# Another layout of the differential attention, with the rotary cosine product on GpSimd

## The reference, cut to what matters

```
q = rope(rms_norm(q, q_g)); k = rope(rms_norm(k, k_g))     # q, k: [tokens, 8 heads, 2, 64]
ky = rms_norm(ky, k_g)                                      # context keys: no rope
s = einsum('bqhcd,bkhcd->bhcqk', q, keys)                   # two components c
p = softmax(s / 8)
a = p[:, :, 0] - lam * p[:, :, 1]
o = einsum('bhqk,bkhe->bqhe', a, vals)                      # vals: 128 wide
out = (rms_norm(o, sub_g) * 0.8).reshape(n, 1024) @ w_o
rope: t1 * cos - t2 * sin, t2 * cos + t1 * sin
```

## Time and profile before

| | us |
|---|---|
| median of 3 runs | 3831.35 (3828.03 to 3834.58) |
| profiled execution, its own time | 3833.75 |
| its span, first to last instruction | 3832.0 |
| PE busy | 3579.2 (93%) |
| DVE busy | 1932.7 (50%) |
| ScalarE busy | 1272.9 (33%) |
| GpSimd busy | 350.1 (9%) |
| mean granted TensorE clock | 0.948 |

### The profile page before, as it was taken

One profiled execution on the slowest core, in us unless ns is written; L12 is line 12 of the kernel. 1 busy time (PEld: TensorE's weight loads), 2 busy tenths in 40 slices (PEclk: granted clock), 3 DMA queues, 4 the chain that ended last, 5 costly groups with the idle time before them and its releaser, 6 DMA issues.

```text
span 3832.0 us, 40505 instructions
## 1 busy us (share of the span) xinstructions
PE 3579.2 (93%) x17064; PEld 2949.4 (77%) x17064; DVE 1932.7 (50%) x2742; ACT 1272.9 (33%) x1771; POOL 350.1 (9%) x200
## 2 busy tenths in 40 slices
PE   2999998899998999899999999989999999999998
PEld 2888887677776888788877888766788877678887
DVE  8434334455555544454444333386564647656464
ACT  4322123333333322322333323333442433344242
POOL 3301001000101000000000000330100023010001
PEclk9999998888888999999999999998899999899999
DMA  5323232000002545354322222220122222012221
GB/s 194 135 84 127 89 116 72 33 28 28 28 34 91 185 147 170 118 173 154 116 77 81 96 99 94 85 79 6 51 98 99 95 77 84 6 50 88 99 94 60
DMA packets 95654, 348.83 MB, mean 91 GB/s; under 512 B 10608, under 2 KB 10864, under 8 KB 94960
## 3 DMA queue, kind: packets, MB, share of 16 engines
q1 hardware_dynamic: 94176, 343.06, 26.2%
q10 hardware_dynamic: 1296, 3.18, 0.2%
HBM read 344.10 MB, written 2.10 MB: 90 GB/s over the span
## 4 chain that ended last, share of the span: by engine, by line
PE 85%; DVE 9%; ACT 3%; POOL 1%; issue 1%; DMA 0%; ACTq 0%; SPq 0%; DVEq 0%; POOLq 0%
PE PS L325 84%; DVE CAC L1689 2%; DVE WL L1319 1%; PE PS L394 1%; DVE ST L1560 1%; ACT WH L845 1%; DVE SCR L1346 1%; POOL SM L1974 1%; ACT G L1012 0%; DVE X L1661 0%; ACT HH L896 0%; DVE ST L1780 0%; ACT G L884 0%; DVE X L1670 0%; POOL PTF L1967 0%
## 5 line engine op out<-in xcount | busy, mean ns | idle before, releaser
L325 PE MATMUL PS<-HH,WH 128*128 128x512 f32 (+1 forms) x3120 | 1204.5, 386 | 58.3 <-DVE HL L1676 18.1
L1319 DVE TENSOR_TENSOR WL<-RAW,WH 128x1024 fp32r<-128x1024 f32 x462 | 576.7, 1249 | 1261.5 <-ACT WH L845 1261.4
L325 PE MATMUL PS<-HL,WH 128*128 128x512 f32 (+1 forms) x3120 | 1187.8, 381 | 0.0
L325 PE MATMUL PS<-HH,WL 128*128 128x512 f32 (+1 forms) x3120 | 1183.1, 379 | 0.0
L845 ACT ACTIVATE WH<-RAW 128x1024 fp32r<-128x1024 f32 x496 | 524.4, 1057 | 1472.7 <-PE PS L325 1460.4
L325 PEld LDWEIGHTS PS<-HH,WH 128*128 128x128 f32 x3120 | 603.0, 193 | 183.7 <-DVE HL L1421 19.4
L325 PEld LDWEIGHTS PS<-HL,WH 128*128 128x128 f32 x3120 | 602.5, 193 | 113.7 <-issue 7.0
L325 PEld LDWEIGHTS PS<-HH,WL 128*128 128x128 f32 x3120 | 599.8, 192 | 111.1
L325 PE MATMUL PS<-AH,WH 128*128 128x512 f32 x1392 | 525.2, 377 | 0.0
L325 PE MATMUL PS<-AL,WH 128*128 128x512 f32 x1392 | 524.8, 377 | 0.0
L325 PE MATMUL PS<-AH,WL 128*128 128x512 f32 x1392 | 523.5, 376 | 0.0
(11 more groups left out here) (266 smaller groups left out, 3321.5 us busy)
## 6 DMA issues: line engine op xcount, KB each, us to landing
RAW<-wst SPq DMA_DIRECT2D x640, 512.0 KB, 3.3
X<-xT SPq DMA_DIRECT2D x1, 2048.0 KB, 12.3
out<-X SPq DMA_DIRECT2D x8, 256.0 KB, 2.0
PTF<-cb SPq DMA_DIRECT2D x1, 1024.0 KB, 4.9
Y<-yT SPq DMA_DIRECT2D x1, 1024.0 KB, 6.3
PTF<-cb ACTq DMA_DIRECT2D x1, 1024.0 KB, 4.8
HM<-sg ACTq DMA_DIRECT2D x4, 256.0 KB, 3.6
ROPE<-rope SPq DMA_DIRECT2D x1, 512.0 KB, 4.2
```

Of the source, the lines that this page charges most:

```text
L325: return e.matmul(o, l, r, start=start, stop=stop)
L1319: e.tensor_tensor(lo, raw_block(s), f32(hi), ALU.subtract).then_inc(*did("dve_done", ("wlo", b)))
```

## The change

PE: the banks of the attention are now given by number (`hold`), not in turn. Scores of a step lie in banks 0 to 2 as one tile of 128x1536; the matmuls of the two components, which use rows 0 to 63 and 64 to 127 of the array, alternate. The turned probabilities (and turned V, and K's spread) use banks 3 and 4, projections bank 5 (K also 6), sums of squares, permutations and spreads of O bank 6, the values' output bank 7. Pieces of the next head are placed anew: K at qt 0 (V's turn in its middle), K's sum, Q and K's permutation at qt 1, Q's sum, a third of V (256 columns), Q's permutation and K's spread at qt 2, the other 512 columns of V at qt 3. The first head starts with K, then Q, then V, and K of head 1 stands ahead of its scores. Cut to the core:

```diff
+            def scores(n):
+                _, prior = hold(("s", n), 768, 0)
+                _, more = hold(("s", n), 512, 2)
+                o = bank["s", n] = PS[:, 0:1536]
...
+                for i, (a, b) in enumerate(((0, 0), (0, 1), (1, 0))):
+                    m = mm(o[:, 512:768], Q[0][a], K[0][b][:, 512:768], i == 0, i == 2)
+                    if i == 2:
+                        m.then_inc(*did("pe_done", ("s bank 1", n)))
+                    mm(o[:, 1024:1536], Q[1][a], K[1][b][:, 256:768], i == 0, i == 2)
+                for i, (a, b) in enumerate(((0, 0), (0, 1), (1, 0))):
+                    m = mm(o[:, 0:512], Q[0][a], K[0][b][:, 0:512], i == 0, i == 2)
...
+                    q.wait_ge("s bank 1", n)
+                    m = mm(o[:, 768:1024], Q[1][a], K[1][b][:, 0:256], i == 0, i == 2)
...
+                if H < 8:
+                    if qt == 0 and n:
+                        project(("k", H), weights(1024, H), 0, NT, 5, True, lambda: turn_values(h))
+                    if qt == 1:
+                        key_stat(H)
+                        project(("q", H), weights(0, H), 0, NX, 5, True, lambda: key_permute(H))
+                    if qt == 2:
+                        query_stat(H)
+                        v = weights(2048, H)
+                        project(("v2", H), v, NX, NT, 5, False, lambda: query_permute(H, 6))
+                        key_spread(H, 3)
+                        if h:
+                            out_stat(h - 1)
+                        if H == 7:
+                            project(("v", H), v, 0, NX, 5)
+                    if qt == 3:
+                        if h:
+                            out_spread(h - 1)
+                        if H < 7:
+                            project(("v", H), v, 0, NX, 5)
```

The tail: output 7 (its first six eighths) stands before the last values; the last two eighths of outputs 0 to 5 run together, with the last sum and spread between their two halves:

```diff
+            turn_p(31)
+            lin([output(7, 0, 6)], oxs(0, 6), [5])
+            values(7, 1)
+            lin([output(m, 6, 8) for m in range(6)], oxs(6, 8), [0, 1, 2, 3, 4, 5], {1: last})
```

DVE: one maximum and one scaling for both components; the negation needs both. The splits of Q and K stand apart from their rotation, and the splits of O 0 to 5 come together at n = 27:

```diff
+            def row_max(n):
+                e.tensor_reduce(s8[:, 0:2], bank["s", n].rearrange("p (c k) -> p c k", c=2), AXX, ALU.max)
+                e.scalar_tensor_tensor(out=s8[:, 2:4], in0=s8[:, 0:2], scalar=-1.0, in1=r, op0=ALU.mult, op1=ALU.mult)
...
                 combine(n)
+                    if qt == 0 and n:
+                        v_split(h)
+                        stream(upto["v", h])
                     if qt == 1:
+                        k_rotate(H)
+                        stream(upto["k", H])
                     if qt == 2:
+                        q_rotate(H)
+                        stream(upto["q", H])
+                        k_scale(H)
+                            stat(("o", h - 1), 1, 4, 1.0 / 128, 1e-6)
+                        k_split(H)
                     if qt == 3:
+                        q_split(H)
+                            o_scale(h - 1)
```

ScalarE: the evictions of the next head stand ahead of the two exponentials of a step, for tiles that PE finished in the step before; the high half of P, weight blocks and splits stand behind them:

```diff
+                if qt == 0 and n:
+                    v_evict(h)
+                    if qt == 1:
+                        k_evict(H)
+                    if qt == 2:
+                        q_evict(H)
+                    if qt == 3:
+                        v_evict2(H)
+                softmax(n)
+                if n:
+                    p_split(n - 1)
```

GpSimd and DVE: the product with the cosine goes from `rope` to GpSimd, in place, behind the permutation that reads the same tile:

```diff
+        def by_cos(key, s):
+            kind, h = key
+            q.wait_ge("rope in")
+            q.wait_ge(kind + "s", h)
+            q.wait_ge("tile", ("p" + kind, h))
+            e.tensor_tensor(s, s, COS, ALU.mult).then_inc(*did("pool_done", ("ropea", key)))
+            def rotate(s, tile, t2, key, done):
+                e.tensor_tensor(t2, bank[tile], SIN, ALU.mult)
+                q.wait_ge("ropeb", key)
+                q.wait_ge("ropea", key)
+                e.tensor_tensor(s, s, t2, ALU.add)
```

More of the change, by code:

```diff
@@ L295, in take @@
             pos += n
[L296 to L299 removed]
+            return hold(name, 512 * n, i)
         def allowed():
@@ L328, in W, with lin @@
             return [((name, l, r0, c0, nr, ncol, dc),)]
-        def lin(tiles, xs):
+        def lin(tiles, xs, into=None, between={}):
             nonlocal released
-            taken = [take(name, N) for name, _, N in tiles]
+            taken = [hold(t[0], t[2], into[i]) if into else take(t[0], t[2]) for i, t in enumerate(tiles)]
             K = len(xs)
             for k, (hi, lo, step, rows) in enumerate(xs):
+                if k in between:
+                    between[k]()
                 for (name, units, N), (bk, prior) in zip(tiles, taken):
@@ L386, in spread, with turn @@
             m.then_inc(*did("pe_done", ("tile", ("sp", name)), ("smfree", name), *more))
-        def turn(name, src, nt, step, *more):
-            bk, prior = take(name, nt * 128)
+        def turn(name, src, nt, step, *more, into=None):
+            bk, prior = take(name, nt * 128) if into is None else hold(name, nt * 128, into)
             q.wait_ge(*step)
             for p in prior:
-                q.wait_ge("free", p)
+                q.wait_ge(*p)
             for t in range(nt):
@@ new lines, in project @@
+            def project(name, us, c0, c1, into, final=True, between=None):
+                nonlocal released
+                bk, prior = hold(name, c1 - c0, into)
+                q.wait_ge("wlo", us[0][2])
+                for p in prior:
+                    q.wait_ge(*p)
+                for k, (hi, lo, step, _) in enumerate(xs):
+                    q.wait_ge(*step)
+                    if k == 4 and between:
+                        between()
+                    for c in range(c0, c1, 512):
+                        d = min(c + 512, c1)
+                        o = bk[:, c - c0:d - c0]
+                        mm(o, us[k][0], hi[:, c:d], k == 0, False)
+                        mm(o, us[k][0], lo[:, c:d], False, False)
+                        m = mm(o, us[k][1], hi[:, c:d], False, k == 7)
+                steps = [("tile", name)]
+                if final:
+                    steps.append(("wfree", us[0][2]))
+                    released += 1
+                m.then_inc(*did("pe_done", *steps))
+                upto[name] = allowed()
@@ L524, in attention @@
-            values(7, 1)
-            stat(("o", 7), [(OSQ, 128, ones, ("osq", 7))], 4, 1)
-            spread(("o", 7), 4, None, ("rs", ("o", 7)), ("attention done",))
-            lin([output(m, 6, 8) for m in range(4)], oxs(6, 8))
-            for m in range(4, 8):
-                lin([output(m, 6, 8)], oxs(6, 8))
+                    turn_p(n - 1)
+                if H < 8:
[18 more added lines that the diff above has]
+                            project(("v", H), v, 0, NX, 5)
+                else:
+                    if qt == 0:
+                        turn_values(7)
+                    if qt == 2:
+                        out_stat(6)
+                    for m in ((0, 1), (2, 3), (4, 5), (6,))[qt]:
+                        lin([output(m, 0, 6)], oxs(0, 6), [5])
+                        if m == 4:
+                            out_spread(6)
@@ L531, in fourier, with last @@
+            turn_p(31)
+            lin([output(7, 0, 6)], oxs(0, 6), [5])
+            values(7, 1)
+            def last():
+                out_stat(7)
+                out_spread(7, ("attention done",))
+            lin([output(m, 6, 8) for m in range(6)], oxs(6, 8), [0, 1, 2, 3, 4, 5], {1: last})
+            for m in (6, 7):
+                lin([output(m, 6, 8)], oxs(6, 8), [m - 6])
         def fourier(xs):
@@ L990, in o_split, with softmax @@
                 e.activation(hview(h, NX)[0], OF[:, h * 512:(h + 1) * 512], ACT.Copy).then_inc(*did("act_done", ("ohi", h)))
-            stream(upto["q", 0])
+            def softmax(n):
+                h, qt = n // 4, n % 4
+                s8 = st8(n)
+                for c in range(2):
+                    use = ("p", n, c)
+                    q.wait_ge("gdone", GBEFORE[use])
+                    q.wait_ge("negmax", n)
+                    steps = [("exp", n, c)]
+                    if c:
+                        steps.append(("free", ("s", n)))
+                        if qt == 3:
+                            steps.append(("smfree", ("q", h)))
+                    e.activation(G(use), bank["s", n][:, c * 768:(c + 1) * 768], ACT.Exp, bias=s8[:, 2 + c:3 + c],
+                                 scale=sm(("q", h), 24 + qt * 2 + c, 1), accum_out=s8[:, 4 + c:5 + c]).then_inc(*did("act_done", *steps))
@@ L1003, in attention @@
             for n in range(32):
[L1004 to L1013 removed]
+                h, qt, H = n // 4, n % 4, n // 4 + 1
@@ L1364, in stat @@
         def stat(name, nsrc, n, inv, eps):
-            sums = PN[:, 0:n]
+            region = bank["st", name]
+            sums = region[:, 0:n]
             q.wait_ge("stat", name)
@@ L1919, in _ @@
         stream(upto["start"])
+        lam()
         norm("f00")
```

422 lines of the change are left out of this document (220 added, 202 removed).

## The result

The changed kernel takes 3765.16 us (median of 4 runs, 3762.93 to 3773.83), the kernel before on the same chip 3830.98 (4 runs). The ratio is 0.9832, 95% interval 0.9814 to 0.9850: 66 us faster, where the forecast was 88. The profiled execution took 3762.93, its span is 3761.1 against 3832.0, and its mean granted clock 0.962 against 0.948. Faster than before is right, 3765 lies in the range, and the size was overstated by 21 us.

What follows compares the result with a forecast made beforehand. It took PE to be the bound, plus a loop from PE to ScalarE and DVE and back. Terms -48.8 - 23 - 7.6 + 2.8 - 11 = -87.6 us, and 2.4 to the median, gave 3744 us from 3833.75; range 3710 to 3788.

Steps and rivals of the forecast that it cites:

- Six heads: Steady heads of the attention: 47.9 us each, 287.4 for six against 336.2, so -48.8.
- Step 2: Third query tile of a head, from its row maximum: DVE's queue sets the end, 13.4 us.
- Step 3: Last query tile of a head: DVE through Q's low half, then the next head's scores on PE, 9.7 us.
- Step 0: First query tile of a head: PE's work 11.9 us plus 1.1 for the low clock, 13.0; DVE covered.
- Step 1: Second query tile of a head: PE 11.0 us, DVE 10.9 and with contention 11.8, which was taken.
- Scores: Score matmuls of a step on PE: alternating row groups overlap, 1.2 us where 1.72 stood before.
- Cosine on GpSimd: Q's product off DVE saves 0.6 in step 2; K's costs DVE 0.9 by contention; net about 0.
- rival of a costly product: GpSimd's product lengthens the DVE operation beside it and may be waited for: +20 us, 3764; chance 0.13.
- Start: Norm to the scores of n=2: K first, vector work hidden under projections; -25 by its terms, -23 taken.
- Head 6 to 7: Steps 26 and 27: V a step earlier, six splits of O together; 28.4 us for 36.06, -7.6.
- Output tiles: Steps 28 to 30: all in bank 5, so the second waits for DVE; 47 us for 44.18, +2.8.
- Tail: Last maximum to sum of squares: output 7 and k=6 halves fill the stretch; 39 us against 49.87, -11.

Runs made afterwards that it cites:

- e10_evict_late: Kernel of e5_v7_step3 with ScalarE's evictions put behind the two exponentials of a step again; 3872.48 us, ratio 1.0111.
- e4_scores_serial: Changed kernel with the twelve score matmuls one component after the other, in the same three banks; 3790.76 us, ratio 0.9893.
- e3_perm_early: Changed kernel with K's permutation ahead of Q's projection instead of in its middle; 3767.95 us, ratio 0.9832.
- e2_cos_dve: Changed kernel with the cosine product back on DVE, new layout kept; 3772.53 us, ratio 0.9846.
- e9_cos_before: Kernel before the change with only the attention's 16 cosine products moved to GpSimd; 3830.49 us beside 3829.91, ratio 1.0001.
- e1_again: The changed kernel timed once more, nothing altered; 3763.99 us, ratio 0.9825.
- e5_v7_step3: Changed kernel with V of head 7 projected in one piece at step 3, as in the other heads; 3761.27 us, ratio 0.9817.
- e6_out_two_banks: Changed kernel with the early output tiles of head 7 in banks 5 and 6 in turn, not 5 alone; 3757.85 us, ratio 0.9807.
- e7_tail_stat: Changed kernel with O's scaling ahead of the combination at n=30, and last outputs' adds and squares ahead of weight blocks; 3764.10 us, ratio 0.9824.
- e8_ends_all: Changed kernel with the edits of e5_v7_step3, e6_out_two_banks and e7_tail_stat together; 3750.45 us, ratio 0.9788.
- e11_tail_four: Kernel of e8_ends_all with the last two eighths of four outputs grouped and four one by one, not six and two; 3748.27 us, ratio 0.9785.
- e12_best: Kernel of e8_ends_all with O's sum in bank 7 and K's scaling ahead of DVE's weight block in step 2; 3749.54 us, ratio 0.9789.

## Why the prediction was right, and where its sizes were off

*The bound and its cure: right.* PE with a loop over ScalarE and DVE was the bound. ScalarE's wait for PE ahead of weight blocks fell from 162.2 to 24.9 us, the clock of the six heads rose from 0.89 to 0.96, and e10_evict_late shows that the gain needs the place of the evictions: with it undone and all else kept, 111 us are gone. No run has early evictions in the old layout, so what that order would give without the fixed banks and the new places of the pieces isn't shown.

*Six heads, -48.8: measured -48.6, in part by luck, as the errors of the steps cancel.* Forecast 13.4, 9.7, 13.0 and 11.8 for steps 2, 3, 0 and 1; measured 12.77, 10.31, 12.39 and 12.21.
- Step 2 is DVE's, as forecast, and 0.6 shorter than the sum of its operations had it (they add up to 13.5). Half of that is the base of every step, 7.5 where 7.83 was charged: from 959.48 to the work behind the combination at 966.99.
- Step 3 was given to DVE's low half of Q. DVE has it done at 980.4, PE ends V at 980.95: PE sets the end.
- Step 0 was charged 1.1 for a low clock. Its granted clock is 1.00; the low stretch falls into step 2 and the start of step 3.
- Step 1 was given to DVE with its contention (11.8, where PE's work was put at 11.0). It is PE's, busy 12.21 of 12.21: the sum of squares takes 1.26 for 0.9, Q with the permutation in its middle 6.58 for 6.05, the scores 1.46 for 1.2. So what DVE and GpSimd do in it costs nothing as long as it ends in time.

*Scores, 1.2: mis-sized, 1.47.* Three of four stand on PE's path, and e4_scores_serial shows how strongly such a difference counts.

*Cosine on GpSimd, net 0: the value is near, the reason wrong.* The forecast had +0.9 of contention on DVE for K and -0.6 for Q. The first didn't come: the permutation is done a good 1 us later in its step than the 7.0 forecast, the product starts at 955.33, 8.1 into it and after the combination, and DVE waits 0.81 for it in a step where it has time. That is the prediction's sign of being wrong, GpSimd as releaser of the rotary sums (5.6 us, 7 times), and it did come, without a price. Moved beside the combination (e3_perm_early) it is GpSimd that is slowed. The second came, -0.60 in step 2 (e2_cos_dve). So the edit is worth some 4 us with the new layout, and nothing in the old one (e9_cos_before). The rival of a costly product had 3764, within 1 us of what was measured, but by coincidence: its cost of 20 us isn't in the six heads, and what is missing lies in the terms behind them.

*Start, -23: measured -24.2.* First maximum at 702.38 (forecast 700.7), that of n=2 at 720.53 (719.5, where its own terms add up to 719.0). In e1_again it comes 1.9 later, so the agreement is good to 2 us and no finer.

*Head 6 to 7, -7.6: failed, -0.5.* The step was "V comes a step earlier and six splits of O stand together". It summed durations and left out that V moved to step 26 needs a tile whose eviction stands in ScalarE's queue behind K's high half. ScalarE in order of time:

```profile
1018.17 0.84 ACT L1051 ACTIVATE QKV<-ACC 128x768 fp32r<-128x768 f32 x1 [5.33 <-DVE ACC L1625]
1018.92 0.37 ACT L1057 ACTIVATE Y<-PS 128x256 f32<-128x256 f32 x1
```

then PE, which waits for that eviction and, ahead of the scores of n=28, for DVE's low half of Q:

```profile
1019.34 0.80 PE L336 MATMUL PS<-HH,WH 128*128 128x512 f32 x1 [2.89 <-ACT Y L1057]
...
1037.02 0.50 PE L336 MATMUL PS<-QKV 64*128 64x256 f32 x2 [4.42 <-DVE QKV L1609]
```

and DVE, whose maximum of n=27 waited for PE, and whose splits of O stand ahead of the maximum of n=28:

```profile
1028.77 1.76 DVE L1657 TENSOR_REDUCE ST<-PS 128x2 f32<-128x1536 f32 x1 [8.77 <-PE PS L336]
...
1037.48 3.69 DVE L1652 TENSOR_TENSOR HL<-OF,HH 128x512 fp32r<-128x512 f32 x6
1041.09 1.75 DVE L1657 TENSOR_REDUCE ST<-PS 128x2 f32<-128x1536 f32 x1
```

PE waits 2.89, then runs V's 24 matmuls in 7.83 (1019.34 to 1027.17, 0.33 each, where the earlier trace rows have 0.23). With V in its old place the 8.0 us are back (e5_v7_step3): the forecast's 28.4 in all would have about held for that version (27.5).

*Output tiles, +2.8: mis-sized, +10.6.* The forecast had 17, 15 and 15 for steps 28, 29 and 30; they took 19.6, 16.8 and 18.4. That bank 5 makes the next tile wait for DVE was forecast, but priced too low; the forecast names neither the wait for V's turn nor the one for GpSimd's power. The waits of PE's matmuls in this stretch, in order of time, V's turn first and O's spread last:

```profile
1046.87 1.11 PE L504 MATMUL PS<-CST,ACC 128*128 128x128 f32 x4 [6.33 <-DVE PTL L1640]
1054.74 0.50 PE L336 MATMUL PS<-HH,WH 128*128 128x512 f32 x1 [0.84 <-DVE X L1676]
1070.12 0.50 PE L336 MATMUL PS<-HH,WH 128*128 128x512 f32 x1 [2.39 <-DVE X L1676]
1086.29 2.07 PE L336 MATMUL PS<-CST,SM 128*128 128x128 f32 x8 [4.28 <-POOL SM L2126]
```

The granted clock over the stretch is 0.84. Two banks take 5.6 us off it (e6_out_two_banks); the scaling of O ahead of the combination takes 2.8 off step 30 in a kernel with one bank (e7_tail_stat), but adds nothing to two (49.51 in e8_ends_all against 49.16). The 6.33 for V's turn stay (6.29 with two banks, 7.84 in e8_ends_all): head 7's step 28 has no K projection left ahead of it to cover DVE's work.

*Tail, -11: mis-sized, -3.2.* The step that failed is the last one, "last outputs and the GpSimd sums", 12.0 us from 24.5 to 36.5. PE, then GpSimd:

```profile
1122.97 0.80 PE L336 MATMUL PS<-HH,WH 128*128 128x512 f32 x1 [2.17 <-DVE HL L1652]
...
1129.79 9.15 POOL L2147 TENSOR_TENSOR ACC<-ACC,G 128x512 f32<-128x512 f32 x6 [10.75 <-ACT G L957]
```

The last outputs start 27.1 after the last maximum instead of 24.5, and from there to the sum of squares it takes 19.6: 6.8 until GpSimd's six sums start, 9.15 for them (1.5 each instead of the 1.3 of a product alone), and 3.6 for PE's two sums, which had waited 7.3 us for GpSimd. Against the forecast 39, with its 2.5 for the low clock, that is 2.6 + 7.6 - 2.5 = 7.7. In e8_ends_all the last outputs start at 24.65, as forecast, and the part behind them is 19.7 all the same; so the 5 us that its 44.4 still lie over 39 are all there. Neither the order of squares and weight blocks nor the group of six shortens it (e7_tail_stat, e11_tail_four); what would is open.

## What to carry to other kernels

In a queue written by hand, put the work whose input the other engine made a step ago first, and the work that waits for this step's result last: in this layout that order was worth more than any operation saved (111 us in e10_evict_late). A piece on the engine that is the last of its step costs its full duration (0.60 in e2_cos_dve), one elsewhere next to nothing; what is taken away there may still be lost to the clock, as in e12_best. So name for each step the instruction without a bracket before moving work to another engine. A sum of durations is good for the steady loop; where the loop ends (the last head, the last tiles) each moved piece needs its own check of what stands ahead of it in every queue.

The fastest versions are those with the three edits for the last head, 3748 to 3750 us, 2.1% under the kernel before; the changes beyond them (e11_tail_four, e12_best) can't be told from it.

## What was not expected of the hardware

*A small delay can come back larger through the clock.* In e4_scores_serial the scores took 0.44 us more and a later low-clock stretch was longer, so that 1.3 us on the path became 3.3 per head. In e12_best heads with the same instructions and the same waits took 46.70 and 49.52. What decides between them, and when such a stretch ends, isn't shown by these runs.

*The unchanged code behind the attention hides gains of a few us.* It is the same in all versions, 11328 matmuls. It took 2618.5 us after the change and 2621.5 in the repeat of the same kernel, 2624.3 in e5_v7_step3 and 2615.3 in e6_out_two_banks. The busy table of e5_v7_step3 over it:

```profile
1135.44:3759.70 2624.26, 2521.00 (x11328) 2047.85 (x11328) 1340.36 (x1887) 888.55 (x1219) 191.36 (x125) 0.96 0.29 96
```

and that of e6_out_two_banks:

```profile
1137.79:3753.10 2615.31, 2511.59 (x11328) 2039.82 (x11328) 1340.40 (x1887) 888.37 (x1219) 191.41 (x125) 0.96 0.29 97
```

PE's busy time differs by 9.4 us for the same matmuls, which is about all of the difference. Time at the lower clock would look so, but the clock column has 0.96 for both and can't show it. One kernel alone differs by 3.0 between two executions, and what the stretch depends on isn't shown. e5_v7_step3 gained 7.5 us in the attention and had 2.8 more here than the repeat of the changed kernel, 5.8 more than its first profile; so its 2.7 in the total say little, and the 7.5 are read from the attention itself.
